# A two-block network on one core: the recurrence's normalisation gathered step by step, gates applied ahead of the norm's factor, an output projection input by input, products moved ahead, and a warm start

## What is computed

```python
def rms_norm(x, g):                       # before each of the stages
    return x * rsqrt(mean(x * x, -1) + EPS) * g
# "per-layer" stage, twice (norms 2 and 5)
gate = sigmoid(rms_norm(x, norm_ple) @ ple_w_gate)
x = x + gate * (p[layer] @ ple_w_proj)    # p: 512 x 256
# recurrent mixer (norm 10), 16 heads of 64
_, y = scan(step, state0, ...)            # done in 4 chunks of 128 tokens
mu, var = mean(y) , mean((y - mu)**2)     # over the 64 of a head
yn = (y - mu) * rsqrt(var + eps) * gn_w + gn_b
bonus = sum(r * k * r_k, head) * v
g = sigmoid(xg @ wg1) @ wg2               # wg2: 160 x 1024
out = ((yn + bonus) * g) @ w_out
```

## Time and profile before

| | us |
|---|---|
| median of 3 runs | 4174.58 (4174.47 to 4175.12) |
| the profiled execution | 4171.64 |
| its span, first to last instruction | 4169.8 |
| PE busy / its weight loads | 4053.7 / 3035.2 |
| DVE / ACT / POOL busy | 1969.1 / 662.6 / 1321.4 |
| mean granted clock of PE | 0.986 of full |

### The profile page before, as it was taken

The page is one execution under the profiler, slowest core; times in us unless marked ns, Lnnn a source line. Parts: engine busy times, 40 slices in busy tenths (PEclk is TensorE's granted clock), DMA queues, the critical chain, the costliest instruction groups (busy, mean ns, idle before and its releaser), DMA issues. The chain is left out here.

```text
span 4169.8 us, 45573 instructions
## 1 busy us (share of the span) xinstructions
PE 4053.7 (97%) x18094; PEld 3035.2 (73%) x18094; DVE 1969.1 (47%) x3503; ACT 662.6 (16%) x1383; POOL 1321.4 (32%) x1134
## 2 busy tenths in 40 slices
PE   8999999998899999999999999999999999999999
PEld 4448888644488885888834588888887447858888
DVE  4536767448377763433245343333324634434432
ACT  2321110114211101100024300010001321201000
POOL 0004434103243441344304344434442061013443
PEclk9999999999999999999999999999999999989999
DMA  3115444210244442222210122222222241112222
GB/s 123 51 60 181 168 172 172 74 67 29 91 172 172 143 170 71 81 91 83 95 51 21 51 81 91 86 76 91 81 86 76 79 119 50 36 41 91 82 86 76
DMA packets 129939, 387.50 MB, mean 93 GB/s; under 512 B 38336, under 2 KB 41408, under 8 KB 120000
## 3 DMA queue, kind: packets, MB, share of 16 engines
q1 hardware_dynamic: 115088, 306.11, 22.2%
q10 hardware_dynamic: 13824, 75.50, 4.8%
q0 software_dynamic: 816, 2.97, 0.2%
HBM read 376.14 MB, written 8.39 MB: 92 GB/s over the span
## 5 line engine op out<-in xcount | busy, mean ns | idle before, releaser
L841 PE MATMUL bank<-normed,weight_ring 128*128 128x256 f32 (+2 forms) x3376 | 1017.1, 455 | 14.5 <-ACT normed L1614 9.3
L841 PEld LDWEIGHTS bank<-normed,weight_ring 128*128 128x128 f32 (+1 forms) x3376 | 637.2, 190 | 358.5 <-issue 274.1
L841 PE MATMUL bank<-area_b,weight_ring 128*128 128x256 f32 (+3 forms) x2032 | 598.6, 441 | 4.1 <-issue 2.8
L841 PEld LDWEIGHTS bank<-area_b,weight_ring 128*128 128x128 f32 (+2 forms) x2032 | 378.7, 187 | 184.6 <-issue 146.3
L749 POOL TENSOR_TENSOR area_d<-weight_ring 128x512 f32<-128x512 f32 (+1 forms) x104 | 130.4, 1254 | 1072.9 <-PE bank L841 924.9
L841 PE MATMUL bank<-area_b 128*128 128x256 f32 (+2 forms) x1680 | 368.0, 376 | 13.4 <-DVE area_b L2695 10.8
L841 PE MATMUL bank<-area_a,weight_ring 128*128 128x256 f32 (+1 forms) x1360 | 373.3, 427 | 0.8 <-DVE area_a L2641 0.7
L841 PE MATMUL bank<-area_b,area_d 128*128 128x256 f32 x1536 | 351.5, 381 | 10.7 <-issue 5.6
L841 PEld LDWEIGHTS bank<-area_b 128*128 128x128 f32 (+1 forms) x1680 | 304.1, 191 | 70.2 <-issue 14.7
L749 POOL TENSOR_TENSOR area_b<-weight_ring 128x512 f32<-128x512 f32 (+1 forms) x104 | 130.5, 1255 | 678.2 <-PE bank L841 653.1
L841 PEld LDWEIGHTS bank<-area_b,area_d 128*128 128x128 f32 x1536 | 292.3, 191 | 53.0 <-issue 13.3
(11 more groups left out here) (310 smaller groups left out, 4998.6 us busy)
## 6 DMA issues: line engine op xcount, KB each, us to landing
weight_ring<-in_weights_dram SPq DMA_DIRECT2D x444, 512.0 KB, 4.6
...
area_b<-in_weights_dram ACTq DMA_DIRECT2D x48, 512.0 KB, 6.4
...
```

Of the source, the lines that this page charges most:

```text
L841: i = pe.matmul(out, lhsT, rhs, start=start, stop=stop)
```

## The change

At the start, the identity and a few columns (144 columns of constants) are loaded right behind x, the rest (2240 columns; unused masks are gone) behind two weight tiles. PE multiplies x's first block with itself five times, unused, as soon as it has landed. ACT begins the squares without waiting for the vectors.

In both per-layer stages the two projection products of the outputs 0, 1 and 2 move into the norm before the stage: four before its sums, two in place of the first filler. They go to banks 4 to 6, and the weights are streamed in that order.

In the recurrence, v is centred over each head by the product that made its transpose (`centre` instead of the identity), so y is centred. ACT also squares y in each step (`step_squares`), PE sums the squares over the features of each head (`square_sum`), and DVE adds them up in `group_variances` (`group_sum`). The last four steps make no state, nor transposed keys. ACT adds gn_b to the bonus beside the first eight steps.

Behind it, the gate's last 32 rows are multiplied on four different row groups of PE, for which ACT's queue copies those rows three times beforehand. DVE multiplies y by the gate and POOL the bonus by the gate; then comes the norm's factor (spread by products of 32 rows, four outputs at a time), and DVE (odd blocks) or POOL (even blocks) adds. The projection's first four outputs are made input by input, and the other four output by output.

```diff
+AHEAD = 3
+PLE_BLOCKS = [10 * j + 8 + k for j in range(AHEAD) for k in range(2)] + [10 * j + k for j in range(AHEAD) for k in range(8)] \
+    + list(range(10 * AHEAD, 80))
...
-    stage(f"ple{n}", 2 * DB, 0, DB * (DB + 2))
+    stage(f"ple{n}", 2 * DB - AHEAD, 0, DB * (DB + 2))
...
+GATE_BLOCKS = [8 * h + b for h in range(2) for b in (0, 2, 4, 6, 1, 3, 5, 7)]
...
+    c["centre"] = c["ident"] - c["halves"] / 64
+    heads, of_heads = np.zeros((P, 2, 32)), np.zeros((P, 2, P))
+    for q in range(2):
+        for e in range(2):
+            heads[64 * e:64 * e + 64, q, 2 * q + e] = 1.0
+            of_heads[2 * q + e::32, q, 64 * e:64 * e + 64] = 1.0
...
-            sp.dma_start(C[:, :], io["constants"]).then_inc(S("constants_landed"), 16)
+            sp.dma_start(C[:, 0:EARLY], io["constants"][:, 0:EARLY]).then_inc(S("first_constants_landed"), 16)
...
+                if n == 2:
+                    sp.dma_start(C[:, EARLY:], io["constants"][:, EARLY:]).then_inc(S("constants_landed"), 16)
...
+            po.wait_ge(S("gn_shifted"), DB)
+
+            def gated_bonus(j):
+                done(po, gn_gate(j))
+                po.tensor_tensor(B[:, 16 + j, :], B[:, 16 + j, :], B[:, j, :], ALU.mult).then_inc(S("bonus_gated"), 1)
+
+            for j in range(4):
+                gated_bonus(j)
+            for j in range(0, DB, 2):
+                po.wait_ge(S("gn_scaled"), j + 1)
+                po.wait_ge(S("bonus_gated"), j + 1)
+                po.tensor_tensor(B[:, j, :], TM[:, j % 4, :], B[:, 16 + j, :], ALU.add).then_inc(S("rw_gated_even"), 1)
+                for i in (j + 4, j + 5):
+                    if i < DB:
+                        gated_bonus(i)
...
+            def ple_ahead(n, j):
+                pe.wait_ge(S(f"p{n // 3}_landed"), 16)
+                part_is_taken(pe, f"down{n - 1}", DB // 2 - 1, ("P7", "P4", "P3")[j])
+                at["w"] = AT[f"ple{n}"][2] + 10 * j + 8
+                for k in range(2):
+                    mm(bank[4 + j][:, :], weight(), PT[:, k, :], k == 0, k == 1, S("ple_projected") if k else None)
...
+                if n in (2, 5):
+                    ple_ahead(n, 0)
+                    ple_ahead(n, 1)
...
-                if 0 < n < 12:
+                if n in (2, 5):
+                    ple_ahead(n, 2)
+                    at["w"] = AT[f"ple{n}"][2]
+                elif 0 < n < 12:
...
+            def project_by_input(rhs, ready, outputs=4):
+
+                w0, ms = at["w"], [product() for j in range(outputs)]
...
+                for k in range(DB):
+                    ready(k)
+                    for j in range(outputs):
+                        tile, b = PLACE[w0 + DB * j + k]
+                        if tile not in seen:
+                            seen.add(tile)
+                            tile_landed(pe, tile)
+                            at["open"] += 1
+                        mm(pbank(ms[j])[:, :], ring[:, tile % RING, b * P:(b + 1) * P], rhs(k), k == 0, k == DB - 1,
+                           product_full if k == DB - 1 else None)
...
+            pe.wait_ge(S("x_landed0"), 16)
+            for _ in range(5):
+                pe.matmul(bank[0][:, :], X[:, 0, 0:P], X[:, 0, :], start=True, stop=True)
+            pe.wait_ge(S("first_constants_landed"), 16)
...
-                    t = pe.transpose(pbank(m)[:, b * P:(b + 1) * P], A[:, 16 + 2 * g + b, chunk(c)], const("ident"))
-                t.then_inc(product_full, 1)
+                    mm(pbank(m)[:, b * P:(b + 1) * P], A[:, 16 + 2 * g + b, chunk(c)], const("centre"), True, True,
+                       product_full if b else None)
...
+            def square_sum(i):
+                s = small()
+                pe.wait_ge(S("gn_square"), i + 1)
+                for b in range(2):
+                    j = 2 * STEPS[i][1] + b
+                    rows = slice(32 * (j % 4), 32 * (j % 4) + 32)
+                    mm(sbank(s)[rows, 0:P], const("heads", j // 4, 32), SQY[:, b, :], True, True, small_full if b else None)
...
-                state(i)
+                if i < 12:
+                    state(i)
...
-                    token_keys(i + 1)
+                    if i + 1 < 12:
+                        token_keys(i + 1)
+                    square_sum(i)
...
-            def mean(j):
-                s = small()
-                mm(sbank(s)[:, :], const("halves"), A[:, j, :], True, True, small_full)
...
-            sums = product()
-            for j in range(DB):
-                pe.wait_ge(S("gn_square"), j + 1)
-                for t in range(NB):
-                    mm(pbank(sums)[:, 16 * t + 2 * j:16 * t + 2 * j + 2], SQ[:, j % 2, t * P:(t + 1) * P],
-                       const("halves")[:, 0:P:64], True, True,
-                       None if t < NB - 1 else S("gn_summed") if j < DB - 1 else product_full)
-                if j + 2 < DB:
-                    mean(j + 2)
...
+            def gates(h, between):
+                ms = []
+                for r in range(4):
+                    if r == 2:
+                        between()
+                    ms.append(product())
+                    at["w"] = w0 + 8 * h + 2 * r
+                    mm(pbank(ms[r])[:, :], weight(), PT[:, 0, :], True, False)
+                at["w"] = w0 + 8 * h + 1
+                w = weight()
+                pe.wait_ge(S("gate_rows_copied"), 48)
+                for r in range(4):
+                    rows = slice(32 * r, 32 * r + 32)
+                    mm(pbank(ms[r])[:, :], w[rows, :], PT[rows, 1, :], False, True, product_full)
+
+            def spreads(h):
+                ss = [small() for r in range(4)]
+                pe.wait_ge(S("gn_rstd"), 2)
+                for r in range(4):
+                    rows = slice(32 * r, 32 * r + 32)
+                    mm(sbank(ss[r])[:, :], const("of_heads", h)[rows, :], GV[rows, :], True, True, small_full)
+
+            gates(0, lambda: square_sum(15))
+            spreads(0)
+            gates(1, lambda: None)
+            spreads(1)
+            at["w"] = AT["rw_out"][2]
             begin("rw_out")
-            for j in range(DB):
-                project(lambda k: B[:, k, :], DB,
-                        (lambda k: done(pe, gn_gate(k))) if j == 0 else settled)
+            y = lambda k: B[:, k, :]
+            project_by_input(y, lambda k: pe.wait_ge(S("rw_gated_odd" if k % 2 else "rw_gated_even"), k // 2 + 1))
+            for j in range(4, DB):
+                project(y, DB, settled)
...
+            act.wait_ge(S("x_landed0"), 16)
+            a(SM[:, 62:63], X[:, 0, 0:1], ACT.Sqrt, scale=0.0)
+            norm(0)
             a(SM[:, 80:88], V[:, VAT["c"]:VAT["c"] + 8, 0], ACT.Silu).then_inc(S("c_act"), 1)
...
+            done(act, rw_in("g", 1))
+            for r in range(1, 4):
+                act.dma_start(PT[32 * r:32 * r + 32, 1, :], PT[0:32, 1, :]).then_inc(S("gate_rows_copied"), 16)
...
+                if i < DB:
+                    sdone(act, rw_in_small("bonus", i))
+                    a(B[:, 16 + i, :], B[:, 16 + i, :], ACT.Identity, bias=vec("rwkv_gn_b", i)).then_inc(S("gn_shifted"), 1)
+                if i == 15:
+                    a(SM[:, 62:63], vec("gn_eps", 0), ACT.Sqrt)
+                    act.wait_ge(S("gn_sum"), 12)
+                    gn_root(slice(0, 3 * P))
+                if i:
+                    sfull(act, RW_SMALL["sum", i - 1])
+                y = pbank(m)[:, 0:256].rearrange("p (b t) -> p b t", t=P)
+                a(SQY[:, :, :], y, ACT.Square).then_inc(S("gn_square"), 1)
+                took(a(A[:, 2 * g:2 * g + 2, chunk(c)], y, ACT.Identity), m)
...
+            def gate_copy(j):
+                full(act, gn_gate(j))
+                took(a(B[:, j, :], pbank(gn_gate(j))[:, :], ACT.Identity), gn_gate(j))
+
+            gate_copy(0)
+            gate_copy(1)
+            act.wait_ge(S("gn_sum"), 16)
+            gn_root(slice(3 * P, T))
+            for j in range(2, DB):
+                gate_copy(j)
...
+            def group_sum(i):
+                c, g = STEPS[i]
+                s = RW_SMALL["sum", i]
+                rows = slice(64 * (g % 2), 64 * (g % 2) + 64)
+                v, part = GV[rows, chunk(c)], sbank(s)[rows, 0:P]
+                sfull(dve, s)
+                if g >= 2:
+                    dve.wait_ge(S("gn_sum"), i - 1)
+                (tt(v, v, part, ALU.add) if g >= 2 else dve.tensor_copy(v, part)).then_inc(S("gn_sum"), 1)
+                dve.wait_ge(S("gn_sum"), i + 1)
+                dve.memset(SM[:, 61:62], 0.0).then_inc(small_done[s % 4], 1)
...
+            dve.wait_ge(S("gn_root"), 1)
+            dve.reciprocal(GV[:, 0:3 * P], GV[:, 0:3 * P]).then_inc(S("gn_rstd"), 1)
...
+            def gated(j):
+                done(dve, gn_gate(j))
+                tt(A[:, j, :], A[:, j, :], B[:, j, :], ALU.mult).then_inc(S("y_gated"), 1)
+
+            def scaled_output(j):
+                s = gn_small("spread", j)
+                sfull(dve, s)
```

(20 more changed lines are left out.)

206 lines of the change are left out of this document (90 added, 116 removed).

## The result

| | before | changed |
|---|---|---|
| median of 4 runs, us | 4174.52 (4173.95 to 4175.12) | 4145.82 (4141.24 to 4147.24) |
| the profiled execution / its span | 4171.64 / 4169.8 | 4144.75 / 4142.9 |
| PE / DVE / POOL busy | 4053.7 / 1969.1 / 1321.4 | 4024.5 / 1971.4 / 1334.7 |
| mean granted clock | 0.986 | 0.988 |

What follows compares the result with a forecast made beforehand. PE, busy 97% of the span, was taken as the bound. Terms -9.5 - 2.5 + 3.6 + 0.7 - 30.4 + 1.0 = -37.1 us gave 4134.5 profiled, 4137.5 as median; range 4125 to 4154.

Steps and rivals of the forecast that it cites:

- the case: Whole kernel: the forecast itself rather than a rival, 4137.5 us, likeliest span 4127 to 4147; chance 0.48.
- rival 1: Behind the recurrence: the row groups don't overlap, so 16 products cost 13.7 instead of 4.4 us; 4147; chance 0.10.
- Rival 2: Behind the recurrence: the clock stays low from the first idle piece on, +6 us; 4143.5; chance 0.22.
- Rival 3: Start: sums at half rate behind the dummies, so 4.8 us gained instead of 9.5; 4142; chance 0.15.
- A: Start: earlier first stream product and faster first output, -9.5 us, bounds -5 and -11.
- B: Two per-layer stages: products moved ahead into the norm, -2.5 us, bounds 0 and -4.
- C: Recurrence: added sums and centring products less removed transposes and state products, +3.6 us, bounds 0 and +8.
- recorded signs: What would show the forecast; in the recurrence, steps of 11.5 us at clock 1.00, the last three near 10.4.
- The 0.7 for ACT's three DMA issues: Ahead of the first gate sigmoids: three DMA issues on ACT add about +0.7 us to DVE's preparation chain.
- D: Normalisation and gates behind the recurrence: output projection starts earlier, -30.4 us after clock charges, bounds -34 and -20.
- E: Output projection: input-by-input order makes the fourth weight tile late, +1.0 us, bounds 0 and +3.
- Rival 4: Recurrence falls to the low clock because each step has waits; slower than before, 4247 us; chance 0.05.

Runs made afterwards that it cites:

- run 2: The changed kernel with v carried to token rows by two transposes instead of two products with the centring matrix, leaving out v's centring; executed once, 4141.45 us.
- run 3: The changed kernel with each of the two sums of squares per recurrence step issued twice, result unchanged; executed once, 4144.97 us.
- run 4: The changed kernel with POOL multiplying only the first column of each bonus block by the gate, so the output differs; executed once, 4142.45 us.

## Why the prediction was right or wrong

The sign, the range and the case were right: what happened is the forecast's, not a rival's, but 8.4 us smaller (28.7 against 37.1). The time alone does not say so: rivals 1 to 3 gave 4147, 4143.5 and 4142, all nearer to 4145.8 than 4137.5 is, and only the traces rule them out. By terms, in the profiled executions (4171.64 to 4144.75, -26.9 where -37.1 was said):

- **A, start, -9.5.** Measured -9.1 in the profiled execution, a median of -8.1 over the nine equal ones (-4.8 to -9.1). The steps were right; the assumption that failed is that each execution finds them alike. Rival 3 (sums at half rate) holds in no execution with dummies; in two of eleven, where PE pauses 1.9 us or more before the sums, the second ones are slower (2.7 and 2.3 us for eight products, 1.9 otherwise).
- **What no term had.** From the first stage to norm 10 the lead changes by -2.6 to +2.4 us from one execution to another, mostly in stages that the change does not touch. In the profiled one it lost 1.25 in the first stage and 2.55 in the second. The median lead at norm 10 is 7.5 us (2.2 to 10.7), where A and B said 12: 4.5 us. I read one execution of before as if its waits were the kernel's. Where the 2.55 comes from is told above, and so is that the first per-layer stage then gives back 1.4 to 1.7 of it; the cause of the wandering behind norm 5 stays open.
- **B, per-layer, -2.5.** -2.1 and +1.0 in the profiled execution, -2.8 together in four others. "Net -0.7 where the norm ran at full clock" came out at -0.69; the extra -1.1 for the first one at -1.4. What was not foreseen is that the norm's clock can also fall in the second one, and that the full 2.1 in the first one comes only behind a loss of 2.5 in the stage before it: without that loss it is 0.4 to 0.75. So part of what B gains in its stage is what the stage before had lost.
- **C, recurrence, +3.6.** This is the term that was mis-sized most: +8.6, just beyond its bound of +8. (The bound was itself worked out too low: a sum of double price adds 15 x 0.40 = 6.0, which gives +9.6.) The recorded signs missed with it: steps of 11.92 us and not 11.5, the last three 10.86 and not 10.4. What is removed was exact: the twelfth step is 11.33 us and the next three 10.86, that is 11.11 + 0.81 less 0.57 and 0.49. What is added was 0.48 and is 0.81 a step. "Ordinary products in place of two transposes: 0.08" was read from four products against two pairs of them; the pair of transposes stood in the earlier trace rows with 0.37 and the pair of products costs 0.64 there (run 2: 0.27 more than transposes). Why a pair costs 0.64 at this place, where two of four in a row take 0.45, no run shows. The sum's 0.40 is 0.34 for itself and 0.19 on its neighbours (run 3). 15 steps by 0.33 are the missing 5.0 us. The 0.7 for ACT's three DMA issues was not found: the lead at the recurrence's start was 7.0 against 6.5 at the stage's first product.
  The Trainium skill, TensorEngine Tiling (Array Packing), Key Properties, says that a change of tiling mode drains the engine; 0.31 paid once and 0.22 for a second pair agree with that, though no run shows the drain by itself. I had given it only the upper bound.
- **D and E, -29.4.** -27.8, and -28.3 by the mean of the five executions with this tail. No run takes this gain apart into its parts (variances collected in the steps, gates ahead of the factor, row groups, the projection input by input); what is checked is the sum's pieces against the rows. Idle pieces of 2.5 and 7.1 were said to be 2.7 and 6.2. Four 32-row products take 1.07 (1.1 said), which ends rival 1. The tile is 1.05 late (1.0 said). The clock's fall costs 3.2 (3.5 said, but 1.5 of it in the second gates, which lost 1.7 in this execution and nothing in the others). Rival 2, the low level throughout from the first pause on, does not hold: the granted clock is 0.74 to 0.83 over the stretches. Windows of the changed kernel from 3647.2 on (PEclk before the last two):
```profile
3647.20:3653.70 6.50, 6.50 (x20) 2.34 (x16) 3.61 (x4) 0.00 (x0) 5.15 (x4) 0.74 0.00 0
3653.70:3660.80 7.10, 0.01 (x2) 0.01 (x1) 6.32 (x11) 2.06 (x4) 5.11 (x3) 0.79 0.00 0
3660.80:3672.00 11.20, 11.18 (x28) 4.62 (x29) 7.56 (x12) 0.00 (x0) 5.95 (x5) 0.83 0.00 0
```
  DVE's multiplies were priced at 0.7, and with POOL at work each took 0.7 to 1.0 or 1.75, since the earlier trace rows show them alone; POOL's own were priced at 1.28 and took 1.7. The Trainium skill, SBUF — State Buffer, Who interferes with whom, says that a DVE instruction with two inputs in SBUF contends with a GpSimd instruction that reads SBUF, and one with at most one such input, outside its two-port modes, doesn't. The traces agree: such multiplies go from 0.69 up to 1.75, while the scalings, whose other operand is in a PSUM bank, stay at 0.75. This rule spoke against the change, and the prediction did not have it; run 4 puts its price on the start of the projection at 1.4 us.
- **The balance.** Executions give 4.5 us less before the recurrence, 5.0 in it and 1.1 behind it; with 0.7 charged for nothing these are 9.9 against the 8.4 between the medians. The 1.5 between is within what single executions differ by.
- **Rival 4** (the recurrence falls to the low clock) does not hold: 3470 to 3640 has PEclk 1.00 with PE busy 169.4 of 170.0 us.
